# Cross attention's scores and values: float32 products become three fp32r products with split operands, and the last head's output is split straight from PSUM

## The reference

```
def cross_attention(h, memn, w_q, w_kv, w_o):
    B, S, D = h.shape
    M = memn.shape[1]
    q = (h @ w_q).reshape(B, S, X_HEADS, X_DH)
    k, v = jnp.split(memn @ w_kv, 2, axis=-1)
    k = k.reshape(B, M, X_HEADS, X_DH)
    v = v.reshape(B, M, X_HEADS, X_DH)
    s = jnp.einsum('bqhd,bmhd->bhqm', q, k, preferred_element_type=jnp.float32) * (X_DH ** -0.5)
    p = jax.nn.softmax(s, axis=-1)
    o = jnp.einsum('bhqm,bmhd->bqhd', p.astype(v.dtype), v).reshape(B, S, D)
    return o @ w_o
```

## Time and profile before

| | |
|---|---|
| median of 3 runs | 2868.69 us (2868.45 to 2870.37) |
| the profiled execution | 2866.0 us |
| its span on the chip | 2864.2 us |
| mean granted TensorE clock | 0.989 |
| PE busy | 2762.2 us, 96% |
| DVE busy | 1029.4 us, 36% |
| ACT busy | 923.6 us, 32% |
| POOL busy | 581.4 us, 20% |

### The profile page before, as it was taken

One profiled execution on the slowest core, in us unless ns is written; L12 is line 12 of the kernel. 1 busy time (PEld: TensorE's weight loads), 2 busy tenths in 40 slices (PEclk: granted clock), 3 DMA queues, 4 the chain that ended last, 5 costly groups with the idle time before them and its releaser, 6 DMA issues.

```text
span 2864.2 us, 34206 instructions
## 1 busy us (share of the span) xinstructions
PE 2762.2 (96%) x13636; PEld 2269.4 (79%) x13636; DVE 1029.4 (36%) x1292; ACT 923.6 (32%) x1469; POOL 581.4 (20%) x246
## 2 busy tenths in 40 slices
PE   7999999999999999999999998899999999999999
PEld 6677788898888887777778887677688888888887
DVE  3544423553313222734534665221323212122223
ACT  4455531112222114433435554233423112021122
POOL 1000012221222223321011224231021222222221
PEclk9899999999999999999999999899999999999999
DMA  3000001111111114121113344320020111111112
GB/s 124 14 13 13 15 22 45 52 45 44 45 44 48 48 51 147 45 91 37 37 44 74 54 84 115 112 66 30 22 66 30 52 45 51 52 44 51 44 52 88
DMA packets 50966, 154.50 MB, mean 54 GB/s; under 512 B 13140, under 2 KB 13396, under 8 KB 50088
## 3 DMA queue, kind: packets, MB, share of 16 engines
q1 hardware_dynamic: 45904, 128.11, 15.2%
q10 hardware_dynamic: 4952, 24.82, 2.3%
HBM read 138.04 MB, written 10.67 MB: 52 GB/s over the span
## 4 chain that ended last, share of the span: by engine, by line
PE 48%; issue 38%; POOL 5%; DVE 3%; ACT 2%; DMA 2%; POOLq 0%; SPq 0%; DVEq 0%; ACTq 0%
PE ps L594 19%; PE ps L675 15%; PE ps L696 4%; POOL w_lo L507 4%; PE ps L1108 2%; DMA w_raw<-in_units 2%; PE ps L1066 1%; PE ps L1257 1%; PE ps L1060 1%; DVE fx_tl L2504 1%; PE ps L1145 1%; DVE stat L2495 1%; PE ps L1282 1%; PE ps L1166 1%; ACT fx_th L1866 1%
## 5 line engine op out<-in xcount | busy, mean ns | idle before, releaser
L507 POOL TENSOR_TENSOR w_lo<-w_raw,w_hi 128x1024 fp32r<-128x1024 f32 x205 | 500.1, 2440 | 2138.8 <-ACT w_hi L1357 2138.6
L594 PE MATMUL ps<-A_hi,w_hi 128*128 128x512 f32 (+1 forms) x1920 | 549.0, 372 | 7.5 <-POOL w_lo L507 1.5
L594 PE MATMUL ps<-A_lo,w_hi 128*128 128x512 f32 (+1 forms) x1920 | 545.3, 370 | 0.0
L594 PE MATMUL ps<-A_hi,w_lo 128*128 128x512 f32 (+1 forms) x1920 | 544.5, 370 | 0.0
L594 PEld LDWEIGHTS ps<-A_hi,w_hi 128*128 128x128 f32 x1920 | 341.8, 189 | 71.5 <-issue 6.2
L594 PEld LDWEIGHTS ps<-A_hi,w_lo 128*128 128x128 f32 x1920 | 343.4, 189 | 61.8
L594 PEld LDWEIGHTS ps<-A_lo,w_hi 128*128 128x128 f32 x1920 | 343.3, 188 | 61.5
L1357 ACT ACTIVATE w_hi<-w_raw 128x1024 fp32r<-128x1024 f32 x205 | 216.2, 1055 | 517.2 <-PE ps L675 331.2
L2572 DVE TENSOR_TENSOR X<-ps,X 128x512 f32<-128x512 f32 x96 | 66.4, 692 | 394.9 <-PE ps L675 317.1
L675 PE MATMUL ps<-w_hi,U_hi 128*128 128x512 f32 x448 | 174.3, 389 | 0.0
L675 PE MATMUL ps<-w_lo,U_hi 128*128 128x512 f32 x448 | 174.3, 389 | 0.0
(11 more groups left out here) (421 smaller groups left out, 4205.7 us busy)
## 6 DMA issues: line engine op xcount, KB each, us to landing
w_raw<-in_units SPq DMA_DIRECT2D x203, 512.0 KB, 3.5
X<-in_x ACTq DMA_DIRECT2D x4, 1024.0 KB, 11.6
X<-in_x ACTq DMA_DIRECT2D x1, 4096.0 KB, 14.9
x_spill<-X ACTq DMA_DIRECT2D x1, 4096.0 KB, 12.2
X<-x_spill ACTq DMA_DIRECT2D x1, 4096.0 KB, 15.9
out<-lnf_xn SPq DMA_DIRECT2D x8, 512.0 KB, 2.6
w_raw<-in_units SPq DMA_DIRECT2D x12, 256.0 KB, 2.5
negm_bc<-negm_rows ACTq DMA_DIRECT2D x4, 512.0 KB, 3.5
```

The lines of the kernel that those rows point to most:

```text
L507: nc.gpsimd.tensor_tensor(w_lo[:, slot, :], w_raw[:, slot, :], w_hi[:, slot, :].bitcast(F32), ALU.subtract).then_inc(w_lo_ready, 1)
L594: last = nc.tensor.matmul(out, w[:, slot, o:o + m], v[:, k, cols] if k is not None else v[:, cols], start=(first and j == 0 and q == 0), s ...
```

## The change

Keys, values, queries and probabilities get a high and a low part, each of type fp32r, and scores and values are computed in three products like all others. The parts are made thus:

- keys: ACT copies `x_kT` to `x_kh` in one instruction of 128x2048 during `w_out`, DVE subtracts to get `x_kl`.
- values: ACT copies the PSUM banks to `x_vh`, DVE subtracts from PSUM to get `x_vl`. PE waits for `x_vl` before the second half of `x_v`. DVE's copy `x_vh` of one head's columns (L2596) is gone.
- queries: ACT copies to `x_qh`, DVE subtracts from PSUM to get `x_ql`; PE waits for `ql`.
- transposed probabilities: ACT copies to `x_th`, DVE subtracts from PSUM to get `x_tl` (`xlow`), eight times a head. PE waits for `tl` instead of `pt`.
- the last head: the six finished tiles of `x_o` are split inside its softmax, and its own two output tiles go from PSUM to `A_hi` and `A_lo` directly.

PE's loop over heads 1 to 3 is written out; ACT and DVE loop over 1 and 2. Some buffers move.

```diff
@@ pe
             for hb in range(2):
-                pe.wait_ge(xa["v"], hb + 1)
+                if hb:
+                    pe.wait_ge(xa["vl"], 1)
                 for kp in range(4):
...
             def xvalues(i, last=False):
 
-                pe.wait_ge(xa["pt"], i * 8 + 8)
-                pe.wait_ge(xa["vh"], i + 1)
+                pe.wait_ge(xa["tl"], i * 8 + 8)
                 for dt in range(2):
                     if not last:
-                        pe.wait_ge(xa["q"], i * 2 + (dt + 3))
+                        pe.wait_ge(xa["ql"], i * 2 + (dt + 3))
+                    cols = slice(i * 256 + dt * P, i * 256 + (dt + 1) * P)
                     for hb in range(2):
-                        for mt in range(2):
-                            ins = nc.tensor.matmul(ps[:, 6 - 2 * dt + hb, :], x_vh[:, mt, dt * P:(dt + 1) * P],
-                                                   x_pT[:, mt, hb * HB:(hb + 1) * HB], start=(mt == 0), stop=(mt == 1))
+                        for x in range(6):
+                            mt = x // 3
+                            v, t = ((x_vh, x_th), (x_vh, x_tl), (x_vl, x_th))[x % 3]
+                            ins = nc.tensor.matmul(ps[:, 6 - 2 * dt + hb, :], v[:, mt, cols], t[:, mt, hb * HB:(hb + 1) * HB],
+                                                   start=(x == 0), stop=(x == 5))
...
-                pe.wait_ge(xa["q"], i * 2 + 2)
-                pe.wait_ge(xa["v"], 3)
+                pe.wait_ge(xa["ql"], i * 2 + 2)
...
-                    for kt in range(2):
-                        last = nc.tensor.matmul(ps[:, qb % 4, 0:256], x_q[:, kt, qb * P:(qb + 1) * P],
-                                                x_kT[:, ds(i * 2 + kt, 1), :].rearrange("p a c -> p (a c)"),
-                                                start=(kt == 0), stop=(kt == 1))
+                    for x in range(6):
+                        kt = x // 3
+                        q, k = ((x_qh, x_kh), (x_qh, x_kl), (x_ql, x_kh))[x % 3]
+                        last = nc.tensor.matmul(ps[:, qb % 4, 0:256], q[:, kt, qb * P:(qb + 1) * P], k[:, 2 * i + kt, :],
+                                                start=(x == 0), stop=(x == 5))
...
                     if qb >= 2:
-                        pe.wait_ge(xa["pt"], i * 8 + (qb - 1))
+                        pe.wait_ge(xa["tl"], i * 8 + (qb - 1))
...
-            with pe.Fori(1, 4) as i:
-                xhead(i, False)
+            for head in range(1, 4):
+                xhead(head, False)
             xvalues(3, last=True)
-            sweep_half("w_xo", "xo", A_hi, A_lo, META, range(ST), lambda o: pe.wait_ge(xa["out"], 8) if o == 4 else None)
+            sweep_half("w_xo", "xo", A_hi, A_lo, META, range(ST), lambda o: pe.wait_ge(sp_lo, SPLIT["xo"] + KT) if o == 4 else None)
@@ act
+            act.wait_ge(xa["k"], KT)
+            fn(x_kh[:, :, :], x_kT[:, :, :], ACT.Copy).then_inc(xa["kh"], 1)
...
                     if qb + 3 < ST:
                         xprob(qb + 3)
+                    if last and qb < 6:
+                        split_hi(x_o, lambda k: act.wait_ge(xa["out"], 6), (qb,))
...
+            xhead(3, False, True)
+            for dt in range(2):
+                act.wait_ge(xa["o"], 7 + dt)
+                fn(A_hi[:, 6 + dt, META:L], pair(3 - dt), ACT.Copy).then_inc(sp_hi, 1)
@@ dve
+            dve.wait_ge(xa["kh"], 1)
+            v.tensor_tensor(x_kl[:, :, :], x_kT[:, :, :], x_kh[:, :, :].bitcast(F32), ALU.subtract).then_inc(xa["kl"], 1)
...
+            for hb in range(2):
+                cols = slice(hb * HB, hb * HB + HB)
+                dve.wait_ge(xa["vh"], hb + 1)
+                v.tensor_tensor(x_vl[:, :, cols], ps[:, 2:4, :], x_vh[:, :, cols].bitcast(F32), ALU.subtract).then_inc(xa["vl"], 1)
+
+            def xhead(i, last=False):
+                for u in range(2):
+                    dve.wait_ge(xa["qh"], i * 2 + (u + 1))
+                    v.tensor_tensor(x_ql[:, u, :], pair(3 - u).rearrange("p a b -> p (a b)"), x_qh[:, u, :].bitcast(F32),
+                                    ALU.subtract).then_inc(xa["ql"], 1)
+
+                def xlow(qb):
+                    cols = slice(qb * P, (qb + 1) * P)
+                    dve.wait_ge(xa["th"], i * 8 + (qb + 1))
+                    v.tensor_tensor(x_tl[:, :, cols], ps[:, 4 + qb % 2, 0:256].rearrange("p (a b) -> p a b", b=P),
+                                    x_th[:, :, cols].bitcast(F32), ALU.subtract).then_inc(xa["tl"], 1)
...
                     if qb + 3 < ST:
                         xmax(qb + 3)
-
-            xhead(0, True)
-            with dve.Fori(1, 4) as i, chain.loop(i - 1, 3, 16):
-                xhead(i, False)
-            split_lo("xo", x_o)
+                    if qb:
+                        xlow(qb - 1)
+                    if last and 1 <= qb < 7:
+                        split_lo_tile("xo", x_o, qb - 1)
+                xlow(7)
+
+            xhead(0)
+            with dve.Fori(1, 3) as i, chain.loop(i - 1, 2, 16):
+                xhead(i)
+            xhead(3, True)
+            for dt in range(2):
+                dve.wait_ge(sp_hi, SPLIT["xo"] + 7 + dt)
+                v.tensor_tensor(A_lo[:, 6 + dt, META:L], pair(3 - dt).rearrange("p a b -> p (a b)"),
+                                A_hi[:, 6 + dt, META:L].bitcast(F32), ALU.subtract).then_inc(sp_lo, 1)
```

More of the change, by code:

```diff
@@ L298, in block_kernel @@
         x_kT = ar("x_kT", 88064, [P, KT, 256])
[L299 to L304, removed]
+        x_kh, x_kl = ar("x_kh", 0, [P, KT, 256], F32R), ar("x_kl", 88064, [P, KT, 256], F32R)
+        x_vh, x_vl = ar("x_vh", 8192, [P, 2, D], F32R), ar("x_vl", 32768, [P, 2, D], F32R)
+        x_qh, x_ql = ar("x_qh", 16384, [P, 2, S], F32R), ar("x_ql", 24576, [P, 2, S], F32R)
+        x_p = ar("x_p", 40960, [P, 4, 256])
+        x_th, x_tl = ar("x_th", 45056, [P, 2, S], F32R), ar("x_tl", 53248, [P, 2, S], F32R)
+        x_o = ar("x_o", 61440, [P, 6, S])
         mem_x = ar("mem_x", 74944, [P, 2, D])
@@ L387, in block_kernel @@
         mem_in = sem("mem_in")
-        xa = {k: sem(f"xa_{k}") for k in ("k", "v", "q", "sc", "nm", "p", "pn", "t", "pt", "vh", "o", "out")}
+        xa = {k: sem(f"xa_{k}") for k in ("k", "kh", "kl", "vh", "vl", "qh", "ql", "sc", "nm", "p", "pn", "t", "th", "tl", "o", "out")}
         ff = {k: sem(f"ff_{k}") for k in ("relu", "sq", "hi", "lo")}
@@ L1270, in xhead @@
                     unit(i * 2 + n0, n0 % 2, 3)
-                    pe.wait_ge(xa["pt"], i * 8)
+                    pe.wait_ge(xa["tl"], i * 8)
                 unit(i * 2 + (n0 + 1), (n0 + 1) % 2, 2)
@@ L1274, in xhead @@
                     xvalues(i - 1)
-                pe.wait_ge(xa["q"], i * 2 + 2)
-                pe.wait_ge(xa["v"], 3)
+                pe.wait_ge(xa["ql"], i * 2 + 2)
+                if first:
+                    pe.wait_ge(xa["vl"], 2)
+                    pe.wait_ge(xa["kl"], 1)
                 def xscores(qb):
@@ L1934, in _ @@
                         lnx.high(5 + kp)
-                fn(x_v[:, :, hb * HB:hb * HB + HB], ps[:, 2:4, :], ACT.Identity).then_inc(xa["v"], 1)
+                fn(x_vh[:, :, hb * HB:hb * HB + HB], ps[:, 2:4, :], ACT.Copy).then_inc(xa["vh"], 1)
             n0 = FIRST["x_heads"]
@@ L1942, in xout, with xhead @@
                 fn(x_o[:, ds(i * 2 + dt, 1), :].rearrange("p a c -> p (a c)"), pair(3 - dt), ACT.Identity).then_inc(xa["out"], 1)
-            def xhead(i, first):
+            def xhead(i, first, last=False):
                 for u in range(2):
                     act.wait_ge(unit_done, i * 2 + (n0 + u + 1))
-                    fn(x_q[:, u, :], pair(3 - u), ACT.Identity).then_inc(xa["q"], 1)
+                    fn(x_qh[:, u, :], pair(3 - u), ACT.Copy).then_inc(xa["qh"], 1)
                     if u == 0:
@@ L1960, in xcopy @@
                     act.wait_ge(xa["t"], i * 8 + (qb + 1))
-                    fn(x_pT[:, :, qb * P:(qb + 1) * P], ps[:, 4 + qb % 2, 0:256].rearrange("p (a b) -> p a b", b=P),
-                       ACT.Copy).then_inc(xa["pt"], 1)
+                    fn(x_th[:, :, qb * P:(qb + 1) * P], ps[:, 4 + qb % 2, 0:256].rearrange("p (a b) -> p a b", b=P),
+                       ACT.Copy).then_inc(xa["th"], 1)
                 for qb in range(3):
@@ L1969, in xhead @@
                         xprob(qb + 3)
+                    if last and qb < 6:
+                        split_hi(x_o, lambda k: act.wait_ge(xa["out"], 6), (qb,))
                 after(n0 + 1, i, 2, 0)
             xhead(0, True)
-            with act.Fori(1, 4) as i:
+            with act.Fori(1, 3) as i:
                 xhead(i, False)
[L1975 to L1978, removed]
+            xhead(3, False, True)
+            for dt in range(2):
+                act.wait_ge(xa["o"], 7 + dt)
+                fn(A_hi[:, 6 + dt, META:L], pair(3 - dt), ACT.Copy).then_inc(sp_hi, 1)
             n0 = FIRST["w_xo"]
```

3 lines of the change are left out of this document (1 added, 2 removed).

## The result

The changed kernel took 2886.89 us (median of 4, 2882.61 to 2888.06) beside 2869.53 for the kernel before (median of 4, 2868.45 to 2872.96): a ratio of 1.0051 [1.0039, 1.0064], 0.5% slower. The profiled execution took 2882.61 us, 16.6 more than the one of before.

The account below looks back on a forecast made before the run. PE bounds queries and values; in softmax PE and DVE wait for each other. -5.7 + 4.35 + 8.85 + 1.25 + 1.25 + 2.9 = +12.9 us gives 2881.6 us, 0.45% slower; range 2875 to 2888.

Parts of the forecast that it names:

- The products: Cross attention on PE: values 24 x 0.227 = 5.44 us, -5.7 us over four heads; 256-wide score products 0.120 us each.
- The rival in which a weight load bounds the 256-wide products: Scores: products take 0.19 us, each head's start is 0.8 later, +5, 2886.4 us; chance 0.02.
- DVE's step: Softmax, heads 0 to 2: xlow adds 0.35, step 1.08 becomes 1.43 us and DVE alone sets the pace; +4.35 us.
- The range's lower end: Whole kernel: 2875 us, from 2878.7 without the clock and xlow at 0.25 instead of 0.35 in 28 steps.
- The rival in which PE stays the bound: Softmax: xlow and splits fit into DVE's free time and waits, -8 us, 2860.7; chance 0.05.
- The last head: Its softmax: the same 1.45, six splits between DVE's steps 6.95, wait for tl 0.45; +8.85 us.
- The waits: PE waits for low parts in head 0's queries and in x_v, each +1.25 us and passed on.
- The clock: PE's granted clock falls after stretches with little work, in x_v and the last head; +2.9 us, bounds 0 and 2 x 1.7.
- The two places: Where the clock was expected to fall: after the second stretch of x_v and after the last head, 1.45 us each.
- the clock falls in heads 0 to 2 too: Behind their last scores PE has too little work; up to three times 1.45 more, 2886.0 us; chance 0.22.
- the stretch of the earlier trace with 1.65 us of work: A 4 us stretch before a clock fall, cited against needing one unbroken gap, which would make the sum 1.45 lower.

Follow-up runs that it names:

- e5: e2 without the low part of the probabilities (eight DVE subtractions a head), the high part read instead: 2862.48 us, 0.9977 of the kernel before.
- e3: Changed kernel with values left in float32, only scores in three products, splits behind the last head: 2870.08 us, 0.9988 of the kernel before.
- e2: Changed kernel with the six splits of finished tiles moved from inside the last head's softmax to behind it: 2880.40 us, 1.0015 of the kernel before.
- e8: Kernel before with only the six splits put inside the last head's softmax, products still float32: 2880.43 us, 1.0037 of the kernel before.
- e4: Changed kernel with extra unread products on PE before its waits for x_vl and x_ql: 2890.36 us, 1.0047 of the kernel before.
- e6: e2 with the factor 1/16 put into the queries and a negated maximum, one DVE instruction fewer per step: 2871.46 us, 1.0006 of the kernel before.
- e1: The changed kernel run again with no edit: 2882.23 us, 1.0034 of the kernel before.
- e7: e3 with the factor 1/16 put into the queries and a negated maximum, one DVE instruction fewer per step: 2867.24 us, 0.9987 of the kernel before.

## Why the prediction was right

The sign, the size and the mechanism came out, at 2886.89 us toward the upper end of the range (2875 to 2888). The terms on the chain, changed kernel less before, make 15.3 us together. The rest of the 16.6 lies ahead of the `x_v` wait: the restart in `w_out` came 2.0 us later, and from there to `x_v` it went 0.7 faster. The terms:

```
                                      predicted   measured
values, heads 0 to 2                  -4.3        -4.2
wait for x_vl                         +1.25       +1.26
clock behind it                       +1.45       +1.6
wait for x_ql, head 0                 +1.25       +1.2
softmax h0 with its unit              +1.45       +2.15
softmax h1, h2, each with its unit    +1.45       +1.81, +2.04
last head's softmax                   +8.85       +8.5
its values, with their clock          +0.0        +0.9
```

**The products.** 24 in 5.44 us, 0.227 each, and the scores 2.17 / 18 = 0.120, as the rows gave. By the Trainium skill ("FP8 and Floating Point Precision", TensorE Precision Notes), with four passes for float32, three products would have made an estimated 5.15; the trace has 5.44. The rival in which a weight load bounds the 256-wide products falls.

**DVE's step.** `xlow` takes 0.33 of a step (0.35 said), but the step is 1.31 and not 1.43. The 1.08 I took for a step without waits held one: from product to maximum it was 0.36 us (1973.12 to 1973.48 before), and in e5 and in the changed kernel it is 0.27. A full DVE does 0.98 + 0.33. Two sizes were off and met: shorter scores give 1.0 us per head (e3), and 0.3 in the unit behind it, where I had 0.4, and `xlow` takes 2.1 (e2 against e5) where 1.45 + 0.4 made 1.85. That they met, and that more falls of the clock filled what was left, is luck; the mechanism is not. (The range's lower end takes 28 steps with `xlow`; six a head and one more at the end, as the prediction counts elsewhere, are 25, which changes it by 0.3 us.) The rival in which PE stays the bound falls: its point was a step of 1.20.

**The last head.** Six splits at 6.79 (e2) and 7.68 (e8) for 6.95 said. The step is 2.45 us (2061.93 to 2064.38 for the product) for 2.6. ACT's high parts are hidden but for the first, whose 0.95 us stands on the chain at 2059.62.

**The waits.** 3.32 and 2.4 us, both passed on in full. In `x_v` the whole chain from wait to first unit moved: PE began `x_heads` 4.24 us later than before, of which 2.63 were there when it began the second half of `x_v` (1892.64 for 1890.01), and the rest is clock. The keys cost nothing, as said: ACT copied them in 1.89 us at 1801.97 and still waited 3.22 for its next load.

**The clock: the step that was mis-sized.** The two places were five: behind `x_v` (1.6), behind head 0's queries, where PE's gap grew from 1.11 to 2.37 us (1.2, by e4's 12.46 for 13.67), behind heads 1 and 2 (22.75 and 22.93 for 21.80: 1.0 and 1.1), and the last head with its values (8.06 for e5's 5.73: 2.3). That makes 7.2 for 2.9, of which the shorter softmax took some back. The rival "the clock falls in heads 0 to 2 too" was thus half of what happened, and the forecast's range reached it. e5 shows that the falls behind heads 1 and 2 come from `xlow`, and what changes with it is that PE has less work between DVE's steps; they need no long gap. But little work is not the whole condition, since e6 has the same work before a held clock and before a fall. The Trainium skill ("TensorE: Matmul & The Clock Gate", Why this matters for your kernels) speaks of idle gaps between bursts of matmuls; here the longest wait on a transposed block in heads 1 and 2 is under a microsecond (e2's longest of 28, the splits taken out, is 0.9), and still the clock falls. Against an unbroken gap the prediction set the stretch of the earlier trace rows with 1.65 us of work, which cannot decide it: in that stretch PE stood idle for 2.35 us in one piece, until 1727.43.

**What stays open.** When the clock falls: the same work went either way in e6, and so did the same wait in `x_v` (last section). And why the restart in `w_out` came 2.0 us later: in e1 it was 1.1, and in other kernels up to 7.7, so most of it is a matter of the execution, but no run ties these 2.0 to a cause. In the last head a small part of 8.5 us may be PE's transposes at the lower clock (0.70 us for two at the end, against 0.44); no run tells it apart from DVE's part.

## What to carry to other kernels

Price a split operand by where its low part is made: one subtraction of 256 columns per block cost 13 us on an engine that had almost no time free between its steps, for products that gave back 5.7, while the scores, whose low parts are made outside the loop, gained. Work that lies hidden behind a stage must not be moved between the steps of an engine that paces it: the same six splits cost nothing behind the last head and 6.8 to 7.7 us inside. The best of these kernels is e7 (scores in three products, values in float32, splits behind, negated maximum), 0.13% faster than the kernel before, and 0.5 to 0.6% than the changed one, by the ratios 0.9987 and 1.0034 to 1.0051. By whole time e3 (0.9988) cannot be told from it; by the stage e7 is 3.6 us shorter.

## What was unexpected of the hardware

Executions of one kernel fall apart early. Near 103 us PE waits for ACT, in code that no kernel here changes, and the length of this wait differs by fractions of a microsecond. The timeline of PE in the kernel before:

```profile
103.32 0.23 PE L841 MATMUL ps<-w_hi,ckv_hi 128*16 128x128 f32 x1 [1.32 <-ACTq L1534]
```

Its window over the next 4 us:

```profile
104.00:108.00 4.00, 4.00 (x29) 3.71 (x29) 3.60 (x3) 2.91 (x4) 0.00 (x0) 1.00 0.00 0
```

The same place in e2, first the timeline:

```profile
103.42 0.23 PE L841 MATMUL ps<-w_hi,ckv_hi 128*16 128x128 f32 x1 [1.95 <-ACTq L1543]
```

and then the window:

```profile
104.00:108.00 4.00, 4.00 (x24) 3.90 (x24) 3.67 (x4) 2.29 (x3) 0.00 (x0) 0.64 0.00 0
```

Behind a wait of 1.32 us the clock held, behind 1.95 it fell to 0.64. Over the ten profiled executions the picture is the same: waits of 1.32 (twice), 1.41 (e5) and 1.51 us (e3) were followed by 1.00, waits of 1.66 (e1) and 1.72 (e8) by 0.78, and waits of 1.95 to 1.97 (e2, e4, e6, e7) by 0.64 to 0.74. PE's restart in `w_out` came at 1801.4 to 1803.5 in the first four and in e1, at 1805.4 in e8, and at 1807.2 to 1809.1 in the last four. That the one follows from the other is not traced. And the same wait can go either way: PE's 2.06 us in `x_v` was followed by a held clock in the kernel before and in e7, and by a fall in e3 and e8.
